# Moving a second weighted one-hot from VectorE to ScalarE, and four more gathered dots per block into the gate table

## What is computed

```python
top_s, top_i = lax.top_k(s, PEER_TOPK)                       # 8 heads, 2 x 128 keys, the best 16 of each
best_s, best_j = lax.top_k(cand_s, PEER_TOPK)                # the best 16 of the 256 pairs
gate = jax.nn.softmax(best_s, axis=-1)
u = expert_u[experts]; v = expert_v[experts]                 # 128 experts a token, of 16384 rows of 1024
act = jax.nn.gelu(jnp.einsum('pd,phkd->phk', xb, u), approximate=False)
return jnp.einsum('phk,phkd->pd', gate * act, v)
```

## Time and profile before

| | |
|---|---|
| median of 3 runs | 3766.74 us (3756.76 to 3779.36) |
| the profiled execution's own time | 3757.52 us |
| its span, first to last instruction | 3755.6 us |
| mean granted clock of TensorE | 0.953 |
| PE / DVE / ACT / POOL busy, share of the span | 90% / 69% / 31% / 23% |
| gate table stage (`block_rows`) | 1719.5 to 2133.5 us of the span |
| rest stage (`rest_rows`) | 2133.5 to 2650 us of the span |

### The profile page before, as it was taken

One profiled execution on the slowest core, in us unless ns is written; L12 is line 12 of the kernel. 1 busy time (PEld: TensorE's weight loads), 2 busy tenths in 40 slices (PEclk: granted clock), 3 DMA queues, 4 the chain that ended last, 5 costly groups with the idle time before them and its releaser, 6 DMA issues. The chain is left out here.

```text
span 3755.6 us, 58665 instructions
## 1 busy us (share of the span) xinstructions
PE 3374.4 (90%) x18867; PEld 3068.5 (82%) x18867; DVE 2585.7 (69%) x4897; ACT 1174.2 (31%) x1966; POOL 873.0 (23%) x900
## 2 busy tenths in 40 slices
PE   5997999786579699999999899999699999999996
PEld 4997999774468599999899899999588888888885
DVE  6435777444358788888888756663577777777775
ACT  3004555321222223226777522222222222222220
POOL 1001111110000001112222257662233333333331
PEclk8998999897789899999999999999899999999998
DMA  6622222242211134445888999994687778778775
GB/s 248 218 88 93 88 88 73 93 125 88 84 54 44 37 123 142 151 155 160 236 235 238 262 308 342 337 332 175 243 296 288 284 287 295 283 283 294 289 284 196
DMA packets 436327, 745.41 MB, mean 198 GB/s; under 512 B 224304, under 2 KB 275680, under 8 KB 433120
## 3 DMA queue, kind: packets, MB, share of 16 engines
q1 hardware_dynamic: 337312, 375.61, 30.1%
q0 software_dynamic: 98304, 368.10, 28.3%
q10 hardware_dynamic: 576, 0.04, 0.0%
HBM read 610.44 MB, written 133.19 MB: 198 GB/s over the span
## 5 line engine op out<-in xcount | busy, mean ns | idle before, releaser
L534 PE MATMUL apab<-h2hi,auhib 128*128 128x384 f32 x2048 | 707.1, 345 | 65.5 <-DVEq L60 47.1
L536 PE MATMUL apab<-h2hi,aulob 128*128 128x384 f32 x2048 | 687.3, 336 | 0.0
L535 PE MATMUL apab<-h2lo,auhib 128*128 128x384 f32 x2048 | 687.3, 336 | 0.0
L1539 POOL DMA_INDIRECT vrow<-in_expert_v,fw_now x256 | 318.1, 1242 | 723.8 <-DVE acc L1565 710.7
L534 PEld LDWEIGHTS apab<-h2hi,auhib 128*128 128x128 f32 x2048 | 387.3, 189 | 75.4 <-ACT ageb L1623 36.6
L535 PEld LDWEIGHTS apab<-h2lo,auhib 128*128 128x128 f32 x2048 | 387.3, 189 | 0.0
L536 PEld LDWEIGHTS apab<-h2hi,aulob 128*128 128x128 f32 x2048 | 386.2, 189 | 0.0
L1623 ACT ACTIVATE ageb<-apab 128x384 f32<-128x384 f32 x256 | 125.7, 491 | 686.9 <-PE apab L536 663.5
L2147 PE MATMUL eheld<-vhi,Hhi 128*128 128x512 f32 x768 | 303.0, 395 | 32.4 <-DVE Hlo L2105 32.4
L1565 DVE SCALAR_TENSOR_TENSOR acc<-vrow,fw_share,acc 128x1024 f32<-128x1024 f32 x256 | 327.2, 1279 | 0.0
L1588 POOL DMA_DIRECT2D aurb<-in_expert_u x128 | 71.6, 560 | 1033.6 <-DVEq L60 709.6
(11 more groups left out here) (295 smaller groups left out, 7419.1 us busy)
## 6 DMA issues: line engine op xcount, KB each, us to landing
aurb<-in_expert_u POOLq DMA_DIRECT2D x128, 512.0 KB, 4.3
vraw<-in_expert_v SPq DMA_DIRECT2D x128, 512.0 KB, 3.3
ahead_dram<-ageb SPq DMA_DIRECT2D x256, 192.0 KB, 3.6
gates_dram<-arena SPq DMA_DIRECT2D x12, 4096.0 KB, 24.0
ga<-ahead_dram SPq DMA_DIRECT2D x128, 384.0 KB, 5.3
gr<-gates_dram SPq DMA_DIRECT2D x128, 384.0 KB, 5.9
late<-in_w_ada SPq DMA_DIRECT2D x48, 512.0 KB, 6.3
gw<-in_w_in POOLq DMA_DIRECT2D x8, 1408.0 KB, 8.7
```

The costliest lines, as they stand in the source:

```text
L534: pe.matmul(out, lhi, rhi, start=(k == 0), stop=False)
L535: pe.matmul(out, lhi, rlo, start=False, stop=False)
L536: return pe.matmul(out, llo, rhi, start=False, stop=(k == n - 1))
L1539: pool.indirect_dma_start(self.ring[i], None, table, bass.IndirectOffsetOnAxis(ap=self.now[:, h, i:i + 1], axis=0)).then_inc(self.row_in[i ...
```

## The change

ScalarE's `last_row` becomes `last_rows`: it writes the last two `row` of a group, by two chained `Abs`, the wait for TensorE, and two `Relu`, of which the second signals. VectorE writes the first two only. `less` holds the negated weights of both. VectorE takes a gathered dot after every second group, eight a block: `ITEMS_GATE` is 96 and `ITEMS_REST` 136, so the rest stage has 17 turns with dots and 11 without. GpSimd issues two batches of four gathers a block, each with one load behind its first gather.

```diff
-ITEMS_GATE = TD // 64 * RING
+ITEMS_GATE = TD // 64 * 2 * RING
@@
-        away, less = sb("gaway", [P, 2, P]), sb("gless", [P, TD // G])
+        away, less = sb("gaway", [P, 2, 2, P]), sb("gless", [P, TD // G, 2])
@@ gpsimd, block_rows
-                        batch = b + ITEMS_BEST // RING
-                        few.choose(pool, batch, half, batch * RING)
-                        for i in range(RING):
-                            few.gather(pool, table, batch, half, i)
-                            if i % 2 == 0:
-                                load(b * 2 + (ROW_GATE + 2 + i // 2), i // 2)
+                        for c in range(2):
+                            batch = b * 2 + (ITEMS_BEST // RING + c)
+                            few.choose(pool, batch, c, batch * RING)
+                            for i in range(RING):
+                                few.gather(pool, table, batch, c, i)
+                                if i == 0:
+                                    load(b * 2 + (ROW_GATE + 2 + c), c)
@@ scalar
-                def last_row(b, gi):
-                    at = bass.ds(b * BT + (gi * G + G - 1), 1)
-                    w = less[:, bass.ds(b * NG + gi, 1)]
-                    link(act.activation(away[:, gi % 2], K.iota[:, :], ACT.Abs, bias=iT[:, at], scale=-1.0))
+                def last_rows(b, gi):
+                    u = gi % 2
+                    for q in range(2):
+                        at = bass.ds(b * BT + (gi * G + G - 2 + q), 1)
+                        link(act.activation(away[:, u, q], K.iota[:, :], ACT.Abs, bias=iT[:, at], scale=-1.0))
                     act.wait_ge(g_mm.sem, g_mm.free(b * NG + gi))
-                    act.activation(row[:, gi % 2 * G + G - 1], away[:, gi % 2], ACT.Relu, bias=wT[:, at], scale=w).then_inc(hot_last.sem, 1)
+                    for q in range(2):
+                        at = bass.ds(b * BT + (gi * G + G - 2 + q), 1)
+                        w = less[:, bass.ds(b * NG + gi, 1), q]
+                        step = act.activation(row[:, u * G + G - 2 + q], away[:, u, q], ACT.Relu, bias=wT[:, at], scale=w)
+                    step.then_inc(hot_last.sem, 1)
@@ vector, block_rows
-                            for q in range(G - 1):
+                            for q in range(G - 2):
...
-                            if gi % RING == RING - 1:
-                                i = gi // RING
-                                few.dot_row(dve, b * RING + (ITEMS_BEST + i), i)
+                            if gi % 2:
+                                i = gi // 2
+                                few.dot_row(dve, b * (2 * RING) + (ITEMS_BEST + i), i % RING)
```

More of the change, by code:

```diff
@@ L1798, in block_rows @@
                         act.wait_ge(st_out[half].sem, st_out[half].free(turn))
-                        last_row(b, 0)
+                        last_rows(b, 0)
                         for gi in range(NG):
                             if gi + 1 < NG:
-                                last_row(b, gi + 1)
+                                last_rows(b, gi + 1)
                             at = half * BT + gi * G
@@ L1830, in _ @@
                 with act.Fori(0, NB // 2) as turn:
-                    link.enter(turn, 2 * NG)
+                    link.enter(turn, 4 * NG)
                     block_rows(turn)
@@ L1845, in turned @@
                     link(dve.tensor_single_scalar(less[:, bass.ds(at * (P // G), P // G)],
-                                                  pt[:, 2].rearrange("p (a q) -> p a q", q=G)[:, :, G - 1], -1.0, ALU.mult), turned_done)
+                                                  pt[:, 2].rearrange("p (a q) -> p a q", q=G)[:, :, G - 2:G], -1.0, ALU.mult), turned_done)
                 def tile(t, at, sparse, first):
```

## The result

The changed kernel takes 3879.07 us (median of 4 runs, 3869.22 to 3891.67) against 3763.36 us before (4 runs): ratio 1.0304, 95% interval 1.0272 to 1.0336. Its profiled execution took 3869.22 us, with a span of 3867.5 us, 111.9 us more than the span before. The forecast was 3870.

The account below looks back on a forecast made before the run. ScalarE was to replace PE as the bound of every gate stage group: +108 us there, -7 rest stage, +8 clock, +109 on 3757.5 gives 3866.5; predicted 3870 us, range 3832 to 3912.

Parts of the forecast that it names:

- The bound moved to ScalarE: Gate stage groups: ScalarE, at 2.40 us a group, becomes the bound above PE's 1.94; PE waits about 0.5 us in each.
- The beat: ScalarE's time per group in the gate stage: from 1.42 us to a sum of 2.43, taken as 2.40.
- The heads and the clock: Gate stage block heads: 1.7 us of ScalarE waiting each; granted clock falls at half of them, +8 us.
- VectorE and the gathers hidden: Gate stage: VectorE's net +6 us is hidden behind ScalarE, and no gather is late.
- Rest stage: Twelve rows of the rest stage lose their 4 dots each: -7 us, bounds 0 and -20.
- The clock falls for good: Rival, 3%: gate stage clock stays at 1.2 GHz, PE's beat 3.9 us, +395 us, 4150 us.
- Pairs overlap more: Rival, 10%: ScalarE's pairs in the gate stage overlap more, 2.2 us a group, stage +70, less 7: 3825 us.
- Not slower: Rival, 3%: added ScalarE work fits its idle time, with a beat below PE's 1.94 us: 3755 to 3768 us.
- Gathers late: Rival, 4%: held gathers make VectorE wait at each batch, about 2 us twice a block, half hidden: +24, 3890 us.

Follow-up runs that it names:

- experiment 1: Changed kernel, but GpSimd's loop, `ITEMS_GATE` and the dots stay as before (4 a block): 3875.27 us, ratio 1.0292 to the kernel before.
- experiment 3: Changed kernel, but ScalarE waits once for both `Abs` of a pair, not after each: 3836.72 us, ratio 1.0183 to the kernel before.
- Experiment 6: Changed kernel, next block's first one-hots on ScalarE ahead of the last copy, last turn behind the loop: 3837.9 us, ratio 1.0212 to before.
- the dots alone: Kernel before with 8 dots a block, doubled `ITEMS_GATE` and the new GpSimd loop; VectorE keeps three one-hots: 3779.16 us, ratio 1.0041.
- experiment 4: Changed kernel with ScalarE's loop over the 12 blocks written out in full: 3815.14 us, ratio 1.0142 to the kernel before.
- experiment 5: Changed kernel, loop kept, but ScalarE's one-hots read block 0's places at constant addresses: 3838.8 us, ratio 1.0195 to the kernel before.
- experiment 10: Changed kernel with three mendings: one wait per `Abs` pair, ScalarE's block loop written out, head hoisted: 3776.42 us, ratio 1.0029 to before.
- experiment 8: Kernel before with ScalarE's next-block one-hots ahead of the last copy and VectorE's block loop written out: 3730.55 us, ratio 0.9902.

## Why the prediction was right

**The bound moved to ScalarE: right, and shown.** Experiments 1 and 3 together: without the dots the stage stays, with 0.24 us less in ScalarE's chain it falls by 41 us, and PE's products start 0.1 us after ScalarE's pair. The claim that ScalarE's spare 110 us do not hold the added 0.94 us a group (2.35 - 1.42 = 0.93 measured) decided the sign, and it could be read off two rows' start times.

**The beat:** 2.40 forecast, 2.35 measured; 192 x 0.05 = 10 us too much. The bound that I had to guess, `Relu` to `Relu`, is inside 0.79 for the pair and the step to the copy, against 0.40 + 0.40. The second chained step, for which I took 0.60 from the heads, was nearer 0.55: the 1.09 us for two is what the earlier trace rows gives twice over. The 0.60 is seen only at the heads, where `Abs` to `Relu` is again 1.17 (1810.37 - 1809.20).

**The heads and the clock:** 1.7 us a block forecast plus 8 us for the clock, 28 in all. Measured: 533.5 - 12 x (16 x 2.35 + 3.4) = 41 us, of which 12.2 are the gaps at the loop's turn, so 29 for what I had listed. PE's idle time at a plain head is 2.70 us (2.8 forecast). Experiment 6 agrees in size: some 27 us for the heads and the clock.

The clock fell at 10 of the 12 heads, where I had said half: at the first, at all five that follow a turn of the loop (5.1 to 5.4 us idle), and at four of the six plain ones. At the plain heads of 2125.85 and 2215.18 the products took 1.15 us and the next ones 1.05, after the same 2.70 us without work. There the fifth products started 9.80 us after the head's first, at the ten others 10.3 to 11.6 us: 11 us in all, an estimate of what the falls cost, against 8 forecast. Nor does the length of the idle time alone decide in the kernel before. The head of the earlier trace rows is not the only one with a fall; the stage's first head (1720.59, after 3.24 us) has one too, and the head at 1861.29 has none after 3.28 us.

**What was missing:** the gaps at the turn of ScalarE's loop, +12 us. ScalarE has no such line before; VectorE had, 11.3 us, and I had read over it. The beat, forecast 10 us too long, and this term, left out, cancelled. That was luck: the stage's +116 against 119.5, and with it the total of +109 against 111.9, are better than their parts.

**VectorE and the gathers hidden: right.** +12 us of VectorE's busy time (6 forecast) made no difference (experiment 1), and no dot waited for a gather in the gate stage. The cover was thin in part: in most of the 50 groups in which the profile names VectorE, its one-hots were ready only 0.14 us before ScalarE's. It names VectorE just as often (48) without the extra dots.

**Rest stage:** -7 forecast, -8.7 measured by the stages of the earlier trace rows; by the experiments' "stage" -10.2, and -8.5 with the dots alone.

**The rivals.** *The clock falls for good:* no; the mean clock is 0.95 in the stage, and once the heads are gone, 0.99, with PE still waiting in every group. The rule of the Trainium skill (TensorE: Matmul & The Clock Gate, A second HAM failure mode) that short idle times between groups make the clock swing does not show in this kernel's groups. *Pairs overlap more:* no in the kernel as it is; the beat of 2.10 exists, but only with one wait or constant addresses (experiments 3 to 5). *Not slower:* it needed a beat under 1.94, and even with three mendings it was 1.99. *Gathers late:* no.

## What to carry to other kernels

Before work is moved to an engine that looks idle, divide its idle time by the number of repeats of the loop that sets the pace, and compare it with the start-to-start cost of what is added: 0.57 us against 0.94 here. The same work cost VectorE 0.26 us a piece. And where an engine writes something short that it then waits for, look at what stands behind the wait: a register address there cost 0.11 us each time, nearly as much again as the wait's 0.14.

## What the runs showed of the hardware that I had not expected

- Waiting for one's own `Abs` and then going on costs 0.43 us from start to start with constant addresses, 0.545 us with an address computed from the loop's register behind the wait (0.86 against 1.09 for two). It was 192 x 0.23 = 44 us here. That the step is what does it is shown by experiment 5. Without a wait the second `Abs` started after 0.29 us, with or without the step (experiments 3 and 10), so the wait alone costs 0.14 us, and the step costs something only behind it.
- An engine stood still at a turn of its loop: ScalarE at all five turns, 2.3 to 2.6 us, once its loop body had two more activations a group; VectorE at four turns before, 2.3 to 3.8 us, and at three in the changed kernel, 3.7 to 4.2 us. Where the loop is written out, the engine has none. The Trainium skill (Runtime: NRT & Kernel Launch, Instruction fetch mechanics) says that a taken branch whose target is no longer held makes the sequencer fetch it by DMA before it can go on. The traces agree as far as they go: of the two queues of kind "instruction" one moved 68 packets in every run, the other 99 in the changed kernel and 76 with ScalarE's loop written out (experiment 4), 68 with the head hoisted in the kernel before and 48 with VectorE's loop written out too (experiment 8). That such a fetch is what the engine waits for is not shown by itself. How long a body may be before it happens no run here measured.
